# A retention, window-attention and product-key-expert step: front work in small pieces, expert diagonals on ScalarE

## The reference, cut to what matters

```python
h = x + concat([retention(q, k, v) * silu(g), window_attention(qs, ks, vs)]) @ w_out
xt = rms_norm(h)
# 8 heads: two halves of 128 key scores each, top 16 of each, top 16 of the 256 sums
s = einsum('thcd,hcnd->thcn', xt @ peer_w_q, peer_sub_keys)
sv, si = top_k(s, 16)
best, sel = top_k(sv[..., 0, :, None] + sv[..., 1, None, :], 16)   # -> idx, 128 experts a token
gates = softmax(best)
a = gelu(einsum('thkd,td->thk', peer_u[idx], xt)) * gates
y = rms_norm(h + einsum('thk,thkd->td', a, peer_v[idx]))
```

## Time and profile before

| | us |
|---|---|
| median of 3 runs | 3551.29 (3551.26 to 3555.35) |
| span of the profiled execution | 3527.6 |
| median less span (start and end around it) | 23.7 |

### The profile page before, as it was taken

How to read it: one execution, slowest core, us unless ns; L and a number is a source line. 1 busy time by engine, 2 the same in 40 slices (tenths; PEclk the granted TensorE clock), 3 DMA queues, 4 the chain that set the end, 5 groups by cost and what they waited for, 6 DMA issues and landing times.

```text
span 3527.6 us, 29191 instructions
## 1 busy us (share of the span) xinstructions
PE 2912.5 (83%) x7730; PEld 1369.6 (39%) x7730; DVE 2267.2 (64%) x5805; ACT 440.9 (12%) x1113; POOL 1245.7 (35%) x1180
## 2 busy tenths in 40 slices
PE   8899997897788878886889778977897788878976
PEld 5566553343333333332344233423443343323332
DVE  2012246669665876578757966696659666875785
ACT  3212110110110011101110101010110110010000
POOL 0000003443444334433444344334443454334342
PEclk9989999998899989998999899989998899989988
DMA  6434139998999889988998899889998999889887
GB/s 220 131 97 137 39 113 407 409 361 316 384 400 383 327 348 407 386 345 335 410 403 337 320 413 410 341 338 380 410 362 308 385 405 385 323 353 379 345 332 294
DMA packets 195511, 1162.35 MB, mean 330 GB/s; under 512 B 20632, under 2 KB 54704, under 8 KB 62288
## 3 DMA queue, kind: packets, MB, share of 16 engines
q0 software_dynamic: 148608, 1082.20, 77.2%
q1 hardware_dynamic: 46800, 79.09, 6.4%
HBM read 1143.48 MB, written 17.87 MB: 329 GB/s over the span
## 4 chain that ended last, share of the span: by engine, by line
PE 44%; DMA 26%; DVE 16%; issue 9%; POOL 3%; SPq 2%; ACT 0%; POOLq 0%; DVEq 0%; ACTq 0%
DMA ring<-in_peer_uv,idxst 25%; PE ps L706 23%; PE ps L451 9%; PE ps L655 6%; DVE ring L1332 5%; PE ps L640 4%; POOL ring L396 3%; DVE ring L1325 2%; DVE proj L1212 2%; DVE proj L1209 1%; DVE proj L1265 1%; DVE proj L1262 1%; DVE proj L1257 1%; DVE proj L1217 1%; PE ps L476 1%
## 5 line engine op out<-in xcount | busy, mean ns | idle before, releaser
L706 PE MATMUL ps<-ring 128*128 128x512 f32 x4096 | 1962.9, 634 | 525.0 <-DVE ring L1325 524.7
L396 POOL DMA_INDIRECT ring<-in_peer_uv,idxst x1024 | 1176.8, 1149 | 1742.1 <-PE ps L706 1547.6
L1332 DVE SCALAR_TENSOR_TENSOR ring<-ring,x2g 128x1024 f32<-128x1024 f32 x1024 | 1233.2, 1223 | 727.6 <-DMA ring<-in_peer_uv,idxst 697.4
L706 PEld LDWEIGHTS ps<-ring 128*128 128x128 f32 x4096 | 809.7, 203 | 1636.4 <-issue 945.7
L945 ACT ACTIVATE small<-small 128x2 f32<-128x2 f32 x516 | 104.1, 203 | 2355.3 <-DVE ring L1332 2345.8
L1325 DVE TENSOR_SCALAR ring<-ident,small,gateg 128x128 f32<-128x128 f32 x1024 | 298.5, 353 | 6.0 <-ACT small L945 5.9
L451 PE MATMUL ps<-ring 128*128 128x352 f32 x896 | 275.9, 468 | 7.5 <-ACT x2g L778 6.7
L655 PE MATMUL ps<-keyw,work 128*128 128x512 f32 (+1 forms) x576 | 253.1, 592 | 0.0
L451 PEld LDWEIGHTS ps<-ring 128*128 128x128 f32 x896 | 172.5, 194 | 106.1 <-issue 10.8
L405 POOL COPY idxg<-idx 128x64 uint32<-128x64 uint32 x16 | 4.1, 258 | 486.5 <-DVE gates L1280 486.4
L655 PEld LDWEIGHTS ps<-keyw,work 128*128 128x128 f32 (+1 forms) x576 | 102.7, 179 | 143.4 <-issue 142.6
(11 more groups left out here) (171 smaller groups left out, 1300.4 us busy)
## 6 DMA issues: line engine op xcount, KB each, us to landing
ring<-in_w_in SPq DMA_DIRECT2D x16, 1408.0 KB, 6.3
ring<-in_peer_uv,idxst POOLq DMA_INDIRECT x1024, 8.6
proj<-proj_scratch SPq DMA_DIRECT2D x7, 1408.0 KB, 10.0
work<-in_wqT SPq DMA_DIRECT2D x16, 512.0 KB, 5.3
h<-in_x_prompt SPq DMA_DIRECT2D x13, 512.0 KB, 4.9
proj_scratch<-x2g SPq DMA_DIRECT2D x28, 176.0 KB, 1.8
proj_scratch<-gfb SPq DMA_DIRECT2D x28, 176.0 KB, 1.8
wo<-in_w_out SPq DMA_DIRECT2D x1, 4096.0 KB, 13.9
```

What stands on the lines that cost most here:

```text
L396: nc.gpsimd.indirect_dma_start(row[r], None, A["peer_uv"], bass.IndirectOffsetOnAxis(ap=idxst[:, col:col + 1], axis=0)).then_inc(ld_row[r] ...
L706: mm = nc.tensor.matmul(acc[:, n * 512:(n + 1) * 512], row_u[r][:, 0:P], row_v[r][:, n * 512:(n + 1) * 512], start=False, stop=False, skip ...
L1332: ins = stt(row_u[r], row_u[r], 1.0, x2g[:], ALU.mult, ALU.mult, accum_out=dot[:, r:r + 1])
```

## The change

All work that was done is still done, in the same forms. What moves:

- Every engine's front is a generator that yields a tick (a number of picks) before each piece. PE and ACT run the pieces that are due after each pair, DVE after each pick. A key-score matmul run of 8 becomes 4 pieces of 2; a ranking pass becomes pieces of 2 to 8 instructions. The pieces of the picking part stand at PICK_AT = 38 and behind.
- The diagonals leave DVE. ACT copies ident x gate into `gdiag` one pair ahead, takes the Gelu, and copies `gdiag` x gelu into the ring buffer, for each pair directly behind its own dots.
- POOL's copies to `idxst` go; it gathers straight from `idxg`, 128 single gathers unrolled. Indices and gates pass through `stage`.
- SP loads the columns of block b+2 as soon as block b+1 is chosen, ahead of the store of block b. DVE's rotation (tick 8) waits for that store (`st_y`).
- The Exp of the window attention is in two halves, with picks between.
- The dynamic DMA scratch is set to 8,192 bytes.

```diff
@@ scalar @@
-            def expert_gelus(b, g):
-                for p in range(PAIRS):
-                    act.wait_ge(dots, ...)
-                    nc.scalar.activation(gel[...], dot[...], ACT.Gelu).then_inc(gelus, 1)
+            def gate_diagonals(p):
+                for side in range(2):
+                    me.did(copy(gdiag[:, p % 2 * 2 + side], ident[:],
+                                scale=gateg[:, p // HPAIRS, (2 * p + side) % HALF:(2 * p + side) % HALF + 1]))
+            def weigh(b, p):
+                r = 2 * p % RING
+                act.wait_ge(dots, b * PAIRS + (p + 1))
+                me.did(nc.scalar.activation(gel[:, r:r + 2], dot[:, r:r + 2], ACT.Gelu))
+                me.sync()
+                for side in range(2):
+                    ins = copy(row_u[r + side][:, 0:P], gdiag[:, p % 2 * 2 + side], scale=gel[:, r + side:r + side + 1])
+                ins.then_inc(diags, 1)
+                ...
+                    gate_diagonals(p + 1)
+                for p in range(EDGE, PAIRS):
+                    weigh(b, p)
+                    due = advance(steps, due, 2 * p + 1)
@@ vector @@
-                for p in pairs:
-                    for r in range(p * PAIR, (p + 1) * PAIR):
-                        ...
-                    if p > pairs[0]:
-                        diagonals(p - 1)
-                diagonals(pairs[-1])
+                for unit in range(2 * EDGE, SLOTS):
+                    expert_dot(b, unit)
+                    due = advance(steps, due, unit)
@@ tensor @@
+            def mixing(b):
+                yield 11
+                ... # q, k transposes
+                yield 13
+                pe.wait_ge(qkT_out, b + 1)
+                ...
+                yield 15
+                pe.wait_ge(stm_ready, b + 1)
+                ... # ret_mm
+                yield 22
+                pe.wait_ge(mixr_ready, b + 1)
+                ... # sw_mm in halves, 31 to 34 window values (sw_o), 36 transposes (mixT_mm)
+            def picking(b, rows, at):
+                yield at
+                ...
+                        if k % 2 and k < KC - 1:
+                            yield at + n * 4 + k // 2 + 1
+                ...
+                yield at + 12
+                pe.wait_ge(x2_ready, b + 1)
+                ...
+                for n in range(4):
+                    yield at + 14 + n * 4
@@ scalar, front @@
+                yield 13 # waits qsT_mm
+                yield 15 # waits ret_mm, then silu
+                yield 29 # Exp of half 0; half 1 at 30
+                yield 33 # waits pT_mm of half 1
+                yield 37 # waits sw_o, mixT_mm
+                yield at + 13 # waits x2T_mm
+                yield at + 22 + half * 8 # waits sc_mm
@@ vector, front @@
+                yield 8 # waits st_y, ld_proj
+                yield 16 # waits ret_mm
+                yield 24 # waits sw_mm, half by half
+                yield 35 # waits sw_o
+                yield at + 8 # waits o_mm
+                for half in range(2):
+                    begin = at + 23 + half * 26
+                    yield from rank_halves(b, half, rows, begin)
+                    yield begin + 11
+                    yield from choose(b, half, rows, begin + 11)
+                    yield from number(b, half, rows, begin + 19)
@@ gpsimd @@
-                            nc.gpsimd.tensor_copy(idxst[:, c0:c0 + RING], idxg[...]).then_inc(staged, 1)
-                            hold(pool, staged, ...)
+                    for unit in range(half * SLOTS // 2, (half + 1) * SLOTS // 2):
+                        hold(pool, used, b * SLOTS + (unit + 1))
+                        fetch(unit % RING, idxg[:, half, unit % HALF:unit % HALF + 1])
@@ sync @@
                 load_residual(b + 1)
+                sp.wait_ge(topk_done, b * 2 + 4)
+                load_columns(b + 2)
                 store_y(b)
-                sp.wait_ge(st_y, b * 16 + 16)
-                load_columns(b + 2)
@@
+PICK_AT = 38
+LAST_AT = 10
-    nc = _bacc.Bacc("TRN2", target_bir_lowering=False, num_devices=1)
+    nc = _bacc.Bacc("TRN2", target_bir_lowering=False, num_devices=1, dynamic_dma_scratch_size=8192)
```

More of the change, by code:

```diff
@@ L81, in leave, with early, advance @@
         self.base, self.n = 0, self.first + turns * self.per
+END = 1 << 30
+def early(q):
+    return 8 + (q - 16) * 9 // 4
+def advance(steps, due, now):
+    while due <= now:
+        due = next(steps, END)
+    return due
 def hold(eng, sem, count):
@@ L694, in add_residual, with front @@
+            def front(b):
+                yield from mixing(b)
+                yield from picking(b, P, PICK_AT)
             def add_residual(b):
@@ L942, in expert_gelus @@
-            def expert_gelus(b, g):
-                for p in range(PAIRS):
-                    act.wait_ge(dots, b * (GROUPS * PAIRS) + (g * PAIRS + p + 1))
-                    nc.scalar.activation(gel[:, p * PAIR:(p + 1) * PAIR], dot[:, p * PAIR:(p + 1) * PAIR],
-                                         ACT.Gelu).then_inc(gelus, 1)
+                for half in range(2):
+                    yield at + 22 + half * 8
+                    act.wait_ge(sc_mm, b * 4 + (2 * half + 2))
+                    copy(proj[0:rows, half * D:(half + 1) * D], FF(2 + 2 * half, 4 + 2 * half)[0:rows, :]
+                         ).then_inc(sc_out, 1)
@@ new lines, in picking, with front, take_gates @@
+                for half in range(2):
+                    yield at + 42 + half * 26
+                    act.wait_ge(best_shift, b * 2 + (half + 1))
+                    part_ = gates[0:rows, half * HALF:(half + 1) * HALF]
+                    nc.scalar.activation(part_, part_, ACT.Exp).then_inc(best_exp, 1)
+            def front(b):
+                yield from mixing(b)
+                yield from picking(b, P, PICK_AT)
+            def take_gates(b, half):
+                act.wait_ge(topk_done, b * 2 + (half + 1))
+                copy(gateg[:, half], stage[:, half, 1]).then_inc(gates_taken, 1)
+                act.wait_ge(gates_taken, b * 2 + (half + 1))
+                act.nop(nofuse=True)
@@ L1116, in sample, with mixing @@
                     tell(sm["st"])
-            def rotation(b):
-                if isinstance(b, int):
+            def mixing(b, mask):
+                first = isinstance(b, int)
+                yield 8
+                if first:
                     v.wait_ge(ld_const, 16 * N_CONST)
                 else:
+                    v.wait_ge(st_y, b * 16)
+                    v.nop(nofuse=True)
                     v.wait_ge(ld_proj, b * 32)
                     v.nop(nofuse=True)
-                rotate(P, proj, rope, work)
+                yield from rotate(P, proj, rope, work)
                 tell(roped)
+                yield 11
                 tt(x2[:, 512:1024].rearrange("p (h e) -> p h e", h=RH),
@@ L1232, in rank_halves, with choose @@
                 hold(v, me.sem, me.base + me.n)
[L1234 removed]
+            def choose(b, half, rows, at):
                 b3 = best[0:rows].rearrange("p (h k) -> p h k", h=HH)
```

596 lines of the change are left out of this document (291 added, 305 removed).

## The result

| | before | changed |
|---|---|---|
| median of 20 runs, us | 3549.98 (3544.07 to 3561.99) | 3555.99 (3552.84 to 3562.38) |
| span of the profiled execution, us | 3527.6 | 3560.6 |

A forecast was written before the change was run, and what follows sets the result against it. DMA bounds the kernel, with losses to PE's dense run and DVE's ranking. Gains of 14 + 2 - 1 = 15 us a block, 7 x 15 + 16 + 2 = 123 in all, give 3428.3 us (3330 to 3540).

The forecast's parts named there:

- Bounds and floor: Whole block: DMA at 2.485 us a pick sets a floor of 324 us; 46 of 370.3 us are lost.
- Diagonals, earlier diagonals: Diagonals move from DVE to ACT, 37 us a block off DVE; buffers given back earlier, worth 0 to 7 us.
- Ranking in pieces: DVE's ranking spread over 52 picks, 2.30 us a pick against 2.485 of DMA; gain 14 us a block (8 to 20).
- Tighter waits: Pieces 0 to 2 picks behind what feeds them: change of -1 us a block (-13 to +6) in picks 8 to 37.
- PE's surplus: Time PE has over in each pick, 0.77 us, taken to absorb most of its idleness from waits.
- the spare: Ring buffers not needed for holding or gathering: 3.2 of 8, 8 us, against 1.8 buffers, 4.5 us, before.
- PE's pieces: Output projection and key scores, picks 38 to 67: same work, 18 us lost against 20; gain 2 (-5 to +9).
- Table loads, store, scratch: Two more ACT table loads a block, 2.6 us; DVE stall of 3 us for the store; smaller DMA scratch 0.
- Start: Before the first block: the first pair is given back earlier, gain 2 us; ACT's later second Exp costs 0.
- Gain spent: Rival: ranking's 14 us come back as bubbles in picks 8 to 52; 3540 us, chance 0.12.
- Spare takes nearly everything: Rival: bubbles and half the PE run vanish in the 8 us of spare; 3330 us, chance 0.16.
- slower: in-step waits: Rival: ten waits at 3.5 us, none taken up, make a block 13 us longer; 3630 us, chance 0.14.

The follow-up runs named there:

- the run with all loosened: The changed kernel with later ticks in all of the front of blocks 1 to 7, same instructions in the same order; 3306.42 us.
- the two parts: The changed kernel with later ticks in blocks 1 to 7, in the picking part only (3468.31 us) or the mixing part only (3389.22 us).

## Why the prediction was wrong

Forecast 3428 (3330 to 3540), measured 3555.99.

- **Bounds and floor.** Right. 2.485 us a pick held wherever nothing else stood in the way (421 GB/s behind the key scores), and the floor of 324 was approached to 10 us.
- **Diagonals, earlier diagonals.** Right, if low. Put at about 0 to 7 us a block beside their share of ranking, they gave 14 to 16 a block when made alone (355.9 against 370.3 and 371.5). A copy in a row takes 0.34 us of ACT (702.6 / 2048) where 0.27 was put, without harm. Landing rose to 11.2 us as the larger spare had it.
- **Ranking in pieces.** Right and mis-sized on the safe side: 14 us forecast, 20 measured by the windows, with no loss left behind the key scores; its pieces do not add 0.3 us a pick there. What ranking costs beside the key scores can't be told apart from PE's run.
- **Tighter waits.** This step failed, and it is nearly the whole miss. The prediction priced 20 to 25 us of PE idleness a block, let PE's surplus and the spare take most of it, and put the change at -1 us for picks 8 to 37 and +2 for PE's stretch. The windows show -12 and -10. The credit is what was wrong: none of the priced idleness shows as taken up. Moving only the ticks gave back 36 us a block (375.8 to 339.7), of which at most 4.7 are PE's wider run. The prices were low for VectorE as well. For ScalarE they came near (12 us put for five waits, 10.9 measured for those and the two score copies). For VectorE 2 to 3.4 us were put for a wait, and the one that was moved by itself cost 4.7. That price counted what VectorE does behind the wait, and left out how long the wait itself is. I counted the 8 us of spare as something that takes up waits. But the spare is used when PE runs behind, and an in-step wait of VectorE lasts until PE has caught up: 18.2 us, over twice the spare. While it lasts no new dots are made, so PE stands idle as soon as it has caught up. This reading fits the rows; what the runs show of it is that one such wait, alone, cost the block more than its whole price. The row that should have told me stood in my own list, 7.46 us for the output projection with half a group between the earlier trace rows.
- **PE's pieces.** Put at 18 us lost, 30 measured in the changed kernel. With loose waits 16 are lost, but over 36 picks: by the same working PE's excess is then 36 x 1.71 + 42.2 - 36 x 2.485 = 14 us, and 16 is that without the 8 us of spare taken off. So PE's density costs what was worked out, the spare did not help here either, and that 16 lies near the 18 is chance. Thinning the work took 5 of them.
- **Table loads, store, scratch.** 60 loads of Gelu's table instead of 48, and they don't explain the miss: the run with all loosened has as many and is 250 us faster. What they cost by themselves was not run. The page of the Trainium skill named there, "ScalarE: Activation LUTs" (Table sets), would have them batched and has about 2.7 us for the load with a drain. The rows here have 1283 ns for a load. Of a drain they show no stretch: in the ACT timeline of block 2 a copy ends at 1449.44, the load stands from 1449.46 to 1450.74, and the next function begins at 1450.75. Dot 8 shows no wait for the store: the 4.7 us ahead of it stand in the rows as issue, and before had them too (4.5). The scratch: 0, as put.
- **Start.** Put at a gain of 2, it was 8 us longer. That trace is the longest: in the nine later runs built on this kernel it ends at 532.9 to 535.9 us, against 529.5 to 529.8 where the front is that of before, so 3 to 8 us. The front's pieces there wait in step as well; no run took it apart.
- **Sums.** ACT's and VectorE's own prices add up to 22 to 29 us, not 20 to 25. "Gain spent" ends by its own 49 against 46 near 3554, not 3540. "Spare takes nearly everything" takes 28 us a block where it has just worked out 31. The range leaves out about 3 in 10 by the chances given, not 2. None of these changes what failed.
- **The rivals.** "Ranking's gain is spent in the waits" is nearest to what happened, at 3540 with a chance of 0.12, and "slower: in-step waits" had the mechanism and nearly the sum: ten waits at 3.5 us, 35 in all, where 36 came back (with more waits loosened than these ten). Its point of decision, 2.2 us each, was passed by prices that I had written down myself. I gave both 0.26 on the ground that PE's 1.27 us of idleness a pair refills the spare. It does so only in stretches without such waits, and there were ten in 54 picks.

## What to carry to other kernels

When work is cut into small pieces and laid between the units of a pipeline, the distance between a piece and what feeds it has to be kept in units of the pipeline, not in pieces: an engine that waits in its queue for another's newest piece also stops the units behind it, and waits for as long as the other is behind. Look for the length of such a wait in the other engine's backlog and not in what follows it; here about half of the length came through as time. Don't count a buffer's spare against its price without a run that shows it: here one such wait cost more than its price, spare or not. Two to four picks of distance turned the same instructions from 3556 into 3306 us, and only then were small pieces better than large ones (3306 against 3415; in step they were at 3556, against 3413 for large ones in the old order).

## What the runs showed that was not expected

- The losses of the two parts added almost exactly (88 + 167 against 250 us), although they share one ring of 8 buffers.
- Ranking at 43 picks, where I had worked out 2.55 us of DVE a pick against 2.485, left DMA full at 421 GB/s once PE's key scores were done, the last 79 us of its 117. DVE was busy for 75.29 of them.
- One wait moved by 4 picks was worth 34 us of 3306.
